# Second expert layer by gathered table rows for one tile of 128 tokens, dense for the other 448

## What is computed

```python
q = (xn @ w_q).reshape(bsz, t, 8, 2, 128)
s = jnp.einsum('bthcd,ckd->bthck', q, sub_keys)           # 128 keys on each of two sides
sv, si = lax.top_k(s, 16)
...                                                        # 16 experts eid of 16384 for each of 8 heads, with gates
hid = jnp.einsum('td,ted->te', xb, u_tab[eb])              # first layer: 128 picked experts per token
out = jnp.einsum('te,ted->td', gelu(hid) * gb, v_tab[eb])  # second layer
h = h + out;  y = rmsnorm(h, final_norm_w)
```

## Time and profile before

| | us |
|---|---|
| median of 3 runs (2453.17 to 2462.32) | 2453.94 |
| profiled execution, its span | 2449.8 |
| stretch 545 to 905 (route) | 360 |
| stretch 905 to 1165 (spread_gates) | 260 |
| stretch 1165 to 1980 (whole groups) | 815 |
| stretch 1980 to 2433 (loaded groups and most of the last) | 453 |
| PE busy, all | 2373.9 (97%) |

### The profile page before, as it was taken

The page is one execution under the profiler, slowest core; times in us unless marked ns, Lnnn a source line. Parts: engine busy times, 40 slices in busy tenths (PEclk is TensorE's granted clock), DMA queues, the critical chain, the costliest instruction groups (busy, mean ns, idle before and its releaser), DMA issues.

```text
span 2449.8 us, 50410 instructions
## 1 busy us (share of the span) xinstructions
PE 2373.9 (97%) x20030; PEld 2323.9 (95%) x20030; DVE 1576.3 (64%) x2909; ACT 955.2 (39%) x1856; POOL 607.8 (25%) x299
## 2 busy tenths in 40 slices
PE   8997888989999999999999999999999999999998
PEld 7996777889999999999999999999999999999998
DVE  5545666576989859997544545444554445777776
ACT  5335554343333349998322222222222222222222
POOL 2434444224454541111311221112211120000000
PEclk9999999999999999999999999999999999999999
DMA  4441111332333326667523232332323323545551
GB/s 175 139 133 41 28 28 32 97 119 89 108 106 108 112 92 195 214 215 237 215 99 118 91 124 96 101 114 92 122 96 105 113 90 115 171 159 188 172 170 66
DMA packets 166063, 299.20 MB, mean 122 GB/s; under 512 B 12144, under 2 KB 103600, under 8 KB 161720
## 3 DMA queue, kind: packets, MB, share of 16 engines
q1 hardware_dynamic: 165944, 297.52, 36.3%
HBM read 233.18 MB, written 64.31 MB: 121 GB/s over the span
## 4 chain that ended last, share of the span: by engine, by line
PE 75%; DVE 2%; issue 1%; ACT 1%; POOL 1%; DVEq 0%; ACTq 0%; POOLq 0%
PE banks L123 23%; PE banks L125 23%; PE banks L124 23%; PE banks L2220 5%; PE banks L1923 1%; POOL u_low L2099 0%; DVE n_y L301 0%; DVE n_sq L342 0%; DVE gates_in L2609 0%; DVE res_lo L308 0%; DVE n_inv L294 0%; DVE gelu_out L2605 0%; DVE onehot_pairs L2308 0%; ACT res_hi L1780 0%; ACT wout_wh L1736 0%
## 5 line engine op out<-in xcount | busy, mean ns | idle before, releaser
L125 PE MATMUL banks<-w_high,v_low 128*128 128x288 f32 x2048 | 604.4, 295 | 0.0
L123 PE MATMUL banks<-w_high,v_high 128*128 128x288 f32 x2048 | 603.9, 295 | 0.4
L124 PE MATMUL banks<-w_low,v_high 128*128 128x288 f32 x2048 | 603.1, 294 | 0.0
L123 PE MATMUL banks<-res_hi,u_high 128*128 128x288 f32 x1456 | 441.6, 303 | 2.8 <-POOL u_low L2099 1.8
L124 PE MATMUL banks<-res_lo,u_high 128*128 128x288 f32 x1456 | 429.6, 295 | 0.0
L125 PE MATMUL banks<-res_hi,u_low 128*128 128x288 f32 x1456 | 429.5, 295 | 0.0
L123 PEld LDWEIGHTS banks<-w_high,v_high 128*128 128x128 f32 x2048 | 384.1, 188 | 3.7 <-DVE w_low L2522 3.7
L124 PEld LDWEIGHTS banks<-w_low,v_high 128*128 128x128 f32 x2048 | 384.1, 188 | 0.1
L125 PEld LDWEIGHTS banks<-w_high,v_low 128*128 128x128 f32 x2048 | 384.2, 188 | 0.0
L2546 DVE TENSOR_TENSOR res_x<-banks,res_x 128x288 f32<-128x288 f32 x496 | 217.9, 454 | 250.5 <-PE banks L125 250.5
L2099 POOL TENSOR_TENSOR u_low<-u_raw,u_high 128x1024 fp32r<-128x1024 f32 x71 | 181.2, 2552 | 686.3 <-ACT u_high L2095 686.3
(11 more groups left out here) (407 smaller groups left out, 4200.5 us busy)
## 6 DMA issues: line engine op xcount, KB each, us to landing
v_raw<-arg_v SPq DMA_DIRECT2D x128, 512.0 KB, 3.8
scratch_gates<-gate_stage SPq DMA_DIRECT2D x18, 2048.0 KB, 7.8
gates_in<-scratch_gates SPq DMA_DIRECT2D x32, 1152.0 KB, 7.1
u_raw<-arg_u SPq DMA_DIRECT2D x35, 1024.0 KB, 5.8
q_raw<-arg_u SPq DMA_DIRECT2D x38, 512.0 KB, 3.6
scratch_hidden<-gelu_ahead SPq DMA_DIRECT2D x56, 288.0 KB, 2.3
gelu_out<-scratch_hidden SPq DMA_DIRECT2D x56, 288.0 KB, 2.8
in_raw<-arg_w_in SPq DMA_DIRECT2D x25, 512.0 KB, 4.6
```

What stands on the lines that cost most here:

```text
L123: pe.matmul(out, ah, bh, start=first, stop=False)
L124: pe.matmul(out, ah, bl, start=False, stop=False)
L125: return pe.matmul(out, al, bh, start=False, stop=last)
```

## The change

The first 128 tokens (SP = 128, tile 0) leave the dense second layer; 448 (DN) stay in it.

- **Row copy.** `v` lies in DRAM group by group. A copy in row order (one contiguous row of 4 KB per expert) is made by 128 DMAs from DRAM to DRAM, one per key: 18 + 20 + 20 + 16 of them in mix, 54 in route, all on SP.
- **Gate matrix** only for 448 tokens: 7 steps instead of 9, so that 14 keys instead of 18 have their first layer there. The gates are stored with tokens innermost, so ACT's copy out of PSUM reads with another stride.
- **First layer as a whole** for 76 keys (72 before) after the gates, for all 576 tokens. DVE multiplies Gelu by gate for the 448 tokens and SP sends each product to DRAM (`scratch_prod`); beside that, the 52 keys whose hidden values are ready are loaded, gated and sent as well. Hidden values of the 128 tokens go to `scratch_hid`.
- **Second layer** after that: for each of 128 keys SP loads v and the product, ACT and DVE split both, PE makes 24 matmuls of 448 columns. The eight slices of the output stay in the eight banks of PSUM over all keys, so the adds of DVE fall away but for eight at the end.
- **Gathered rows.** `place_picks` on DVE makes index lists for the 128 tokens. POOL issues 128 indirect DMAs for the hidden values (one element per token each) and 128 for rows of v (128 rows of 4 KB each), into a ring of 16; DVE weighs and adds them with 128 SCALAR_TENSOR_TENSOR of 128x1024, between the splits of keys 9 to 121. Then it norms and transposes these rows, and SP stores them in 16 DMAs of runs of 128 bytes.
- **End.** The last three keys are ordered by output slice; norm and scaling of all 448 tokens follow the last slice. Loops of experts are written out.

```diff
+SP = P
+DN = TOK - SP
+NB = DN // TB
+G_STEPS = DN // (2 * TB)
...
-FETCH = 256
+MIX_COPIES = (0, 18, 38, 58, N_KEYS - (2 * P_HEADS + AHEAD4))
...
+        self.v_rows = VRows(self)
+        self.hid = nc.dram_tensor("scratch_hid", (N_KEYS, P, SP), F32, kind="Internal").ap()
+        self.prod = nc.dram_tensor("scratch_prod", (N_KEYS, P, DN), F32, kind="Internal").ap()
+        self.gates = a["gates"].rearrange("g p t j -> g p (t j)")[:, :, 0:DN * JJ].rearrange(
+            "g p (n j t) -> g p n j t", j=JJ, t=TB)
...
+    def copy(self, sp, k0, k1):
+        for k in range(k0, k1):
+            q = D_MODEL // 4
+            sp.dma_start(self.dst[k].rearrange("p (q d) -> p q d", q=4),
+                         self.src[k // JJ][:, :, k % JJ * q:(k % JJ + 1) * q]).then_inc(self.copied, 16)
+
+    def ready(self, eng):
+        eng.wait_ge(self.copied, 16 * N_KEYS)
...
+                core.v_rows.copy(sp, MIX_COPIES[0], MIX_COPIES[1])
...
+                        core.v_rows.copy(sp, MIX_COPIES[i + 1], MIX_COPIES[i + 2])
...
+                    sp.dma_start(core.hid[KEY4 + n], gelu[:, n % 2, 0:SP]).then_inc(gelu_sent[n % 2], 16)
...
+                core.v_rows.copy(sp, MIX_COPIES[-1] + j, MIX_COPIES[-1] + j + 1)
...
+                link(dve.tensor_reduce(gsum[:, 0, 0:1], own, AX_X, ALU.add))
+                link(dve.scalar_tensor_tensor(out=left[:, 1, :], in0=picks[:, 0, 1, :], scalar=float(N_KEYS),
+                                              in1=picks[:, 0, 0, :], op0=ALU.mult, op1=ALU.add))
+                link(dve.tensor_scalar(left[:, 2, :], left[:, 1, :], float(SP), gsum[:, 0, 0:1], ALU.mult, ALU.add))
...
...
-        stage = core.sb("gate_stage", [P, 2, NG, TB, JJ], ctx=ctx)
+        stage = core.sb("gate_stage", [P, 2, NG, JJ, TB], ctx=ctx)
...
-                    src = core.psum[:, g % BANKS, :].rearrange("p (t g j) -> p g t j", t=FOUR, j=JJ)
-                    act.activation(stage[:, b, :, r * FOUR:(r + 1) * FOUR, :], src, ACT.Copy).then_inc(staged, 1)
+                    src = core.psum[:, g % BANKS, :].rearrange("p (t g j) -> p g j t", t=FOUR, j=JJ)
+                    act.activation(stage[:, b, :, :, r * FOUR:(r + 1) * FOUR], src, ACT.Copy).then_inc(staged, 1)
...
+RING = 16
+CHUNK = 16
+V_SLOTS, W_SLOTS, G_SLOTS, H_SLOTS, M_SLOTS = 4, 3, 3, 3, 4
+NC_KEYS = KEY4
+TAIL = 3
+FIRST_OUT = NC_KEYS - W_SLOTS
+ACC_FROM, ACC_TO = 9, 122
...
-        def out(pe, g, par):
...
-                for jj in range(JJ):
-                    if k == 0:
-                        pe.wait_ge(w_low, g * JJ + jj + 1 + 2)
-                    w = slice(jj * QW + dt % 2 * P, jj * QW + dt % 2 * P + P)
-                    cols = slice(half * HALF, (half + 1) * HALF)
-                    ins = three_products(pe, o, vh[:, q, w], vl[:, q, w], wh[:, par, jj, cols],
...
-        def add_out(dve, g, q):
...
-                x = acts.x[:, k // 2, (k % 2) * HALF:(k % 2 + 1) * HALF]
-                dve.wait_ge(out_done, g * OUTS + k + 1 + O2)
-                dve.tensor_tensor(x, core.psum[:, 4 + k % 4, 0:HALF], x, ALU.add).then_inc(out_added, 1)
...
+        def load_w(sp, k):
+            m = place[k]
+            sp.wait_ge(made_sent[m % M_SLOTS], 16 * (m // M_SLOTS + 1))
+            if k >= W_SLOTS:
+                sp.wait_ge(w_low, k - W_SLOTS + 1)
+            sp.dma_start(w_raw[:, k % W_SLOTS, :], core.prod[k]).then_inc(w_in[k % W_SLOTS], 16)
...
+        def product(pe, k, dt):
+            w = slice(dt * P, (dt + 1) * P)
+            return three_products(pe, out_bank(dt), vh[:, k % V_SLOTS, w], vl[:, k % V_SLOTS, w], wh[:, k % W_SLOTS, :],
+                                  wl[:, k % W_SLOTS, :], k == 0, k == N_KEYS - 1)
+        def pe_out(pe):
+            for k in range(N_KEYS - TAIL):
+                pe.wait_ge(v_low, k + 1)
+                pe.wait_ge(w_low, k + 1)
+                for dt in range(DT):
+                    if k == 0 and dt == 2:
+                        pe.wait_ge(rows_out, 1)
+                    if k == 0 and dt == 4:
+                        pe.wait_ge(gelu_done, NC_KEYS)
+                    ins = product(pe, k, dt)
                 ins.then_inc(out_done, 1)
-
...
+        def split_w_high(act, k):
+            act.wait_ge(w_in[k % W_SLOTS], 16 * (k // W_SLOTS + 1))
+            if k >= W_SLOTS:
+                act.wait_ge(out_done, k - W_SLOTS + 1)
+            act.activation(wh[:, k % W_SLOTS, :], w_raw[:, k % W_SLOTS, :], ACT.Copy).then_inc(w_high, 1)
...
+        def make(dve, key, src, gate):
+            m = place[key]
+            if m >= M_SLOTS:
+                dve.wait_ge(made_sent[m % M_SLOTS], 16 * (m // M_SLOTS))
+            dve.tensor_tensor(blocks(made[:, m % M_SLOTS, :]), blocks(src), gate, ALU.mult).then_inc(made_done, 1)
...
+        def accumulate(dve, s):
+            if s % CHUNK == 0:
+                weigh(dve, s // CHUNK)
+            dve.wait_ge(row_in[s % RING], 16 * (s // RING + 1))
+            if s:
+                dve.wait_ge(summed_rows, s)
+            else:
+                dve.wait_ge(rows_out, 1)
+            dve.scalar_tensor_tensor(out=total[:, :], in0=ring[:, s % RING, :], scalar=sparse.weight[:, s:s + 1],
+                                     in1=total[:, :] if s else rows[:, :], op0=ALU.mult, op1=ALU.add).then_inc(summed_rows, 1)
...
+        def dve_out(dve):
+            done = 0
+            for k in range(W_SLOTS, N_KEYS):
+                split_v_low(dve, k)
+                split_w_low(dve, k)
+                due = min(SEL, max(0, (k - ACC_FROM + 1) * SEL // (ACC_TO - ACC_FROM)))
+                for s in range(done, due):
+                    accumulate(dve, s)
+                done = max(done, due)
+            finish_rows(dve)
...
+            for b in range(4):
+                for j in range(4):
+                    sp.dma_start(a["y"][32 * j:32 * j + 32, :, 32 * b:32 * b + 32], q[32 * b:32 * b + 32, :, j, :]).then_inc(
+                        stored, 16)
...
+        def pool_rows(pool):
+            def value(s):
+                pool.indirect_dma_start(
+                    out=sparse.value[:, s:s + 1], out_offset=None, in_=core.hid.rearrange("k p t -> (k p t)").unsqueeze(1),
+                    in_offset=bass.IndirectOffsetOnAxis(ap=sparse.hidden[:, s:s + 1], axis=0)).then_inc(
+                        values_in[s // CHUNK], 16)
+
+            def row(s):
+                if s >= RING:
+                    pool.wait_ge(summed_rows, s - RING + 1)
+                pool.indirect_dma_start(
+                    out=ring[:, s % RING, :], out_offset=None, in_=core.v_rows.dst.rearrange("k p d -> (k p) d"),
+                    in_offset=bass.IndirectOffsetOnAxis(ap=sparse.expert[:, s:s + 1], axis=0)).then_inc(row_in[s % RING], 16)
...
+            pool.wait_ge(hid_done, NC_KEYS)
+            for s in range(CHUNK):
+                value(s)
+            for s in range(SEL):
+                row(s)
+                if s + CHUNK < SEL:
+                    value(s + CHUNK)
 ```

630 lines of the change are left out of this document (327 added, 303 removed).

## The result

The changed kernel took 2282.4 us (median of 4 runs, 2273.95 to 2299.02), the kernel before 2453.56 beside it: a ratio of 0.9305, 95% interval 0.9264 to 0.9345. The forecast was 2206, inside its range of 2190 to 2300 but 76 us too low. The profiled execution has a span of 2285.1 us, where 2202.0 was summed up.

The account below looks back on a forecast made before the run. PE was taken to bound the kernel, busy for 97% of the span. From 2449.8 us, -230.4 - 53.8 + 25.4 + 3 + 2 + 6 = -247.8 gave a span of 2202.0, forecast as 2206 us, range 2190 to 2300.

Parts of the forecast that it names:

- (a): Second layer's matmuls: fp32r really runs at the rate of 288 columns in 132.5 ns; +49 us, 2255; chance 0.14.
- (b): Gates: ACT's strided copy out of PSUM makes ACT the bound; +11 to +37 us, about 2230; chance 0.16.
- (c): Second layer: gathered rows come too slowly, by POOL (+91, 2297) or the DMA engines (+128, 2334); chance 0.12.
- Term 1: Second layer: 3072 matmuls of 448 columns at 0.190 us, assuming a floor under short matmuls; saves 230.4 us.
- Term 5: Second layer's followers: DVE, ACT, loads and POOL's gathers stay hidden behind PE's 4.56 us per key; 0 us.
- c: Second layer: cost of one indirect DMA on POOL, taken as about 1.3 us, enough while below 2.0.
- The prediction's own alarm: Second layer: the prediction is wrong if PE's waits there sum to more than 20 us.
- Rival (d): Second layer: POOL's indirect DMAs shut DVE out, slower than before; at 1.5 us each +258, 2464; chance 0.06.
- Term 2: Gates: two steps go, -53.8 us; their four keys move to the first layer as a whole, +25.4.
- Term 3: First layer as a whole: 6.36 us a key, with a stall at its start, +3 us, bounds 0 and 8.
- Term 4: Row copies in mix and route: only the last 16 stand before something, the w_out load; +2 us.
- Term 6: End: norm and scaling now all follow the last add, 16 us against 10.9; +6 us, bounds 3 and 15.

Follow-up runs that it names:

- e7: Changed kernel with POOL paced and second-layer keys 50 to 79 cut to 384 down to 128 columns; 0.1735 us a matmul at 384, 0.1317 at 288, floor 0.111.
- e4: Changed kernel with 20 row copies instead of 74 in mixing and two instead of one per projection-stage job; 2232.9 us.

## Why the prediction was right, and where not

The time lies in the range by luck in part. The upper part of the range stood for (a), (b) and half of (c). Of these only (a) came, by 39 of its 49 us; the other 47 us are a hole that neither a term nor a rival names.

**Term 1, the size.** "I take a floor, and for 448 columns ... 0.190 us": the step that failed. The spacing is 0.2027 (51 of them from 1611.26 to 1621.60), +39 us over 3072. This is nearly rival (a), 0.206, which had a chance of 0.14. The evidence taken against (a), 512-column records on plain float32, spoke of another data type; e7 shows one slope for fp32r from 288 to 448. The half-clock row was read rightly and holds at 448 too:

```profile
1673.05 0.57 PE L127 MATMUL banks<-w_low,v_high 128*128 128x448 f32 x1
1673.42 0.57 PE L128 MATMUL banks<-w_high,v_low 128*128 128x448 f32 x1
```

0.37 us, 448 columns at 1.2 GHz with nothing added. But it does not follow that the surcharge at full clock is a floor: a rate of 0.44 ns per column that only full clock meets fits both. A rate and a floor could not be told apart from one width, and the likelier value should have been the mean of the bounds, or (a) given far more than 0.14.

**Term 5, the hole.** "0" was right for every part it costed, and the sum is out by 47 us for one it did not have. c came out at 0.95 + 0.30 = 1.25 where DVE leaves it alone (taken: 1.3). From 1700 to 2100 us:

```profile
L2782 POOL DMA_INDIRECT row_ring<-scratch_v_rows,expert_of_pick x93 | 153.7, 1652 | 129.1 <-DVE row_total L2710 116.0 <-issue 13.1
...
L2710 DVE SCALAR_TENSOR_TENSOR row_total<-row_ring,weight_of_pick,row_total 128x1024 f32<-128x1024 f32 x93 | 119.2, 1282 | 1.4
L2665 DVE TENSOR_TENSOR v_low<-v_raw,v_high 128x1024 fp32r<-128x1024 f32 x82 | 99.8, 1217 | 0.0
```

The row operation takes 1.28 (taken: 1.39), v_low 1.22 as before; POOL waits for DVE, not DVE for rows: rival (c) is out. DVE's three operations sum to 270.9 us in 400, 3.30 a key (taken: 3.44) of 4.86; the DMA share is 0.85 at 278 GB/s (taken: 0.87 at 295). What nobody had asked is what POOL does when nothing holds it: it runs ahead until its ring is full, 61 us without a pause, and PE, which waits for none of it, pays. The prediction's own alarm, waits of PE above 20 us in the second layer, went off for that, though not for the waits that it meant: PE waited for w_low once, for 0.3 us, from 1680 us on.

**Rival (d)** is out, and its direction was the wrong way round: an indirect DMA does not stretch DVE; beside DVE's v_low it takes 1.68 us instead of 0.95, beside the row operation up to 1.94 (the row above has the mean, 1.65). The Trainium skill, SBUF — State Buffer, "Who interferes with whom", infers that a `tensor_tensor` and the preparing of a DMA do not meet; here they do, at POOL's cost. Whether that is by the preparing or by the 128 indices that POOL reads, no run tells.

**Term 2** held: -54.0 for -53.8, parts still 1.68 us apart, and **rival (b)** fell, though the Trainium skill's cacheline rule (Advanced Engine Details and Errata, Memory Cachelines) spoke for it. ACT's copy with elements 512 bytes apart costs what the packed one did:

```profile
L2321 ACT ACTIVATE gate_stage<-banks 128x512 f32<-128x512 f32 x112 | 65.8, 587 | 5.2 <-PE banks L2279 3.7
```

**Term 3** held in kind: Gelus at 1126.08, 1133.30, 1140.06, 1148.35 and 1154.71, then 6.36 apart to 1599.91. Its stall of 3.2 us replaced one of 3.6 in the kernel before (eight Gelus from 1164.21 to 1212.33), so +3 should have been 0.

**Term 4** failed in its place. "Only the last 16 stand in front of something": the 16 copies took 23.1 us of SP's queue, so w_out was issued 34 us later, and its cover of 49.7 us held: it was used 10.5 us later, and everything was late by as much already. SP's loads of the last tile stood at 390.61 instead of 379.90. The stage runs slower beside the copies, tile by tile (see e4); +10.7 where +2 was taken, of which e4 gives back some 8. By what, the engines' operands, the loads or the clock (0.93 beside 0.97 above), is not settled. **Term 6**: +4.4 for +6.

With 39 + 47 + 9 in, and 3, 1.6 and 1.2 (route) out, the 2202.0 become 2291; the span was 2285.1, and the 6 us between are those named above.
